# Token-major projections in chunks of 512 columns, in a transformer kernel of eleven stages on one core

## The reference

```
# first block, layer 0 (mix_0) and layer 1 (mix_1)
qa, ka, va, qb, kb, vb = jnp.split(xn @ w_in, splits, axis=-1)    # va: 256 columns, vb: 768
q, k, v = jnp.split(xn @ w_in, 3, axis=-1)                        # v: 1024 columns
# second block (mix_2)
hq, hf, hi, hgt, nq, kc, vc, ksl, vsl, kwn, vwn, ngate = jnp.split(h @ w_in[l], offsets, axis=-1)
                                                  # hi: 512, vsl and vwn: 128 each, ngate: 24 columns
```

## Time and profile before

| | |
|---|---|
| timed runs, median of 3 | 3481.54 us (3477.34 to 3484.66) |
| profiled execution, its span from first to last instruction | 3476.3 us |
| PE busy in it | 3343.7 us, 96% |
| DVE, ACT, POOL busy | 1999.1, 1753.2, 1211.2 us |
| mean granted clock of TensorE | 0.985 of full |
| `v_ab`, `v_c`, `tok_2` in the span | about 502 to 582, 1624 to 1671, 2341 to 2393 us |

### The profile page before, as it was taken

How to read it: one execution, slowest core, us unless ns; L and a number is a source line. 1 busy time by engine, 2 the same in 40 slices (tenths; PEclk the granted TensorE clock), 3 DMA queues, 4 the chain that set the end, 5 groups by cost and what they waited for, 6 DMA issues and landing times.

```text
span 3476.3 us, 49224 instructions
## 1 busy us (share of the span) xinstructions
PE 3343.7 (96%) x16800; PEld 2705.7 (78%) x16800; DVE 1999.1 (58%) x2493; ACT 1753.2 (50%) x2114; POOL 1211.2 (35%) x625
## 2 busy tenths in 40 slices
PE   8999999999999999999999999899889999999996
PEld 6888888678888788888678888688766788787774
DVE  4335672663354433541463333457776699888888
ACT  5552212645533555321545533423563688888883
POOL 3444441044444444444134444342203222222224
PEclk9999999999999999999999999999999999999998
DMA  3225321023244222443422233222002899999997
GB/s 125 96 95 171 112 100 37 2 85 97 97 150 141 85 97 97 151 132 110 128 72 95 96 94 103 76 95 82 31 1 77 333 402 414 408 410 401 393 397 307
DMA packets 128103, 555.40 MB, mean 160 GB/s; under 512 B 19344, under 2 KB 19600, under 8 KB 100112
## 3 DMA queue, kind: packets, MB, share of 16 engines
q1 hardware_dynamic: 112896, 520.59, 41.5%
q0 software_dynamic: 14976, 33.58, 2.6%
q10 hardware_dynamic: 144, 0.08, 0.0%
HBM read 531.62 MB, written 41.94 MB: 165 GB/s over the span
## 4 chain that ended last, share of the span: by engine, by line
PE 60%; issue 25%; POOL 7%; DVE 5%; ACT 2%; DMA 1%; POOLq 0%; DVEq 0%; SPq 0%; ACTq 0%
PE ps L731 17%; PE ps L733 16%; PE ps L732 16%; POOL w_lo L1762 7%; PE ps L1189 2%; PE ps L751 1%; PE ps L892 1%; PE ps L1268 1%; PE ps L917 1%; PE ps L902 1%; PE ps L1018 1%; PE ps L1000 1%; PE ps L979 0%; DMA big<-in_exp_gu 0%; PE ps L1208 0%
## 5 line engine op out<-in xcount | busy, mean ns | idle before, releaser
L1762 POOL TENSOR_TENSOR w_lo<-stage_buf,w_hi 128x1024 fp32r<-128x1024 f32 (+1 forms) x396 | 971.8, 2454 | 1554.9 <-ACT w_hi L1344 1554.9
L1344 ACT ACTIVATE w_hi<-stage_buf 128x1024 fp32r<-128x1024 f32 (+1 forms) x396 | 413.9, 1045 | 1254.9 <-PE ps L733 1204.8
L731 PE MATMUL ps<-x_hi,w_hi 128*128 128x512 f32 x1984 | 776.1, 391 | 8.7 <-POOL w_lo L1762 7.9
L732 PE MATMUL ps<-x_lo,w_hi 128*128 128x512 f32 x1984 | 774.9, 391 | 0.0
L733 PE MATMUL ps<-x_hi,w_lo 128*128 128x512 f32 x1984 | 774.5, 390 | 0.0
L731 PE MATMUL ps<-hid,w_hi 128*128 128x512 f32 x1312 | 519.0, 396 | 2.6 <-issue 1.7
L733 PE MATMUL ps<-hid,w_lo 128*128 128x512 f32 x1312 | 511.7, 390 | 0.0
L732 PE MATMUL ps<-hid,w_hi 128*128 128x512 f32 x1312 | 510.8, 389 | 0.0
L731 PEld LDWEIGHTS ps<-x_hi,w_hi 128*128 128x128 f32 x1984 | 374.2, 189 | 90.7 <-POOL w_lo L1762 9.6
L733 PEld LDWEIGHTS ps<-x_hi,w_lo 128*128 128x128 f32 x1984 | 374.3, 189 | 78.0
L732 PEld LDWEIGHTS ps<-x_lo,w_hi 128*128 128x128 f32 x1984 | 374.2, 189 | 77.5
(11 more groups left out here) (388 smaller groups left out, 5121.8 us busy)
## 6 DMA issues: line engine op xcount, KB each, us to landing
stage_buf<-in_gu SPq DMA_DIRECT2D x176, 512.0 KB, 3.3
big<-in_exp_gu SPq DMA_DIRECT2D x72, 1024.0 KB
h_buf<-in_exp_gu SPq DMA_DIRECT2D x72, 1024.0 KB
s_buf<-in_exp_dn SPq DMA_DIRECT2D x72, 1024.0 KB
slot_rows<-stage_buf SPq DMA_DIRECT2D x72, 512.0 KB
stage_buf<-in_down SPq DMA_DIRECT2D x64, 512.0 KB, 3.6
stage_buf<-in_down SPq DMA_DIRECT2D x32, 384.0 KB, 3.1
sil_buf<-in_ada SPq DMA_DIRECT2D x24, 512.0 KB, 4.1
```

The source lines that it names most:

```text
L731: nc.tensor.matmul(o, a_hi, b_hi, start=start, stop=False)
L732: nc.tensor.matmul(o, a_hi, b_lo, start=False, stop=False)
L1344: nc.scalar.activation(w_hi[s][:, 0:n], stage[s][:, 0:n], ACT.Copy).then_inc(upper_done, 1)
L1762: nc.gpsimd.tensor_tensor(w_lo[s][:, 0:n], stage[s][:, 0:n], w_hi[s][:, 0:n].bitcast(F32), ALU.subtract).then_inc(parted, 1)
```

## The change

The widths of the chunks come from a table: `v_ab` is cut in 256, 512 and 256 columns, `v_c` in 512 and 512, `tok_2` in 512 and 280 (the 256 value columns and the 24 gates, without the padding). A unit of a wide chunk holds two feature tiles and 512 (or 280) columns, so a wide chunk takes four units, and each unit feeds 24 matmuls. There are still eight units in each phase, of the same size. The `by_class` reading of the stationary operand stays as it is. PE's and DVE's waits count by the table. In mix_2 DVE has two evacuations instead of four, and the 24 gate columns are copied right behind the 256 value columns, ahead of `hgrn_keys`.

```diff
@@ -69,6 +69,18 @@
     PHASES += [(f"gu_{_l}_1", 2 * NF), (f"down_{_l}_1", KD * len(DOWN)), (f"pg_{_l}", 8), (f"pp_{_l}", 2)]
 PHASES += [("in_2", 20), ("tok_2", 8), ("cmp", 8), ("out_2", 8), ("shared", 6)]
 WHOLE = ("cmp", "shared")
+
+
+V_WIDTHS = {"v_ab": [256, 512, 256], "v_c": [512, 512], "tok_2": [512, 280]}
+CHUNKS = {}
+for _name, _widths in V_WIDTHS.items():
+    CHUNKS[_name], _at = [], 0
+    for _c, _w in enumerate(_widths):
+        _deep = 4 if _w == 256 else 2
+        CHUNKS[_name].append(dict(width=_w, deep=_deep, first=_at, units=KD // _deep, col=sum(_widths[:_c]),
+                                  by_class=_name == "v_ab" and _c > 0))
+        _at += KD // _deep
+    assert _at == 8
 BASE, CUT = {}, {}
 _at = _cut = 0
 for _name, _n in PHASES:
...
@@ -810,27 +822,25 @@
 
             def token_major(phase):
 
-                U, units = BASE[phase]
-
-                def some(x, k, t, c):
-                    if phase == "v_ab" and c > 0:
-                        return by_class(x[:, k, :])[:, t, :]
-                    return x[:, k, t * P:t * P + P]
-
-                for c in range(units // 2):
-
-                    pe.wait_ge(evac_done, U + 2 * c)
+                U = BASE[phase][0]
+                for c, ch in enumerate(CHUNKS[phase]):
+                    width, deep, first = ch["width"], ch["deep"], ch["first"]
+
+                    pe.wait_ge(evac_done, U if c == 0 else U + 2 + CHUNKS[phase][c - 1]["first"])
                     if c == 1 and phase == "tok_2":
                         pe.wait_ge(std_ready, NORM_N["first"] + 1)
                     if c == 1 and phase in ("v_ab", "v_c"):
                         pe.wait_ge(rcol_ready, 1 if phase == "v_ab" else 2)
-                    for s in range(2):
-                        pe.wait_ge(parted, CUT[phase] + 2 * c + s + 1)
-                        wh, wl = tiles(w_hi[s], 256), tiles(w_lo[s], 256)
+                    for n in range(ch["units"]):
+                        s = (first + n) % 2
+                        pe.wait_ge(parted, CUT[phase] + first + n + 1)
+                        wh, wl = (tiles(w[s][:, 0:deep * width], width) for w in (w_hi, w_lo))
                         for t in range(TT):
-                            for kk in range(KD // 2):
-                                k = 4 * s + kk
-                                last = three(ps[:, 4 * ((c + 1) % 2) + t, 0:256], some(x_hi, k, t, c), some(x_lo, k, t, c),
+                            for kk in range(deep):
+                                k = deep * n + kk
+                                hi, lo = (by_class(x[:, k, :])[:, t, :] if ch["by_class"] else x[:, k, t * P:t * P + P]
+                                          for x in (x_hi, x_lo))
+                                last = three(ps[:, 4 * ((c + 1) % 2) + t, 0:width], hi, lo,
                                              wh[:, kk, :], wl[:, kk, :], k == 0, k == KD - 1)
                         last.then_inc(units_done, 1)
 
...
@@ -2042,22 +2052,25 @@
                         ins = nc.vector.tensor_scalar(o, a, scale, None, ALU.mult)
                     ins.then_inc(evac_done, 1)
 
-            def token_units(phase, first, n, dst, pitch, width=256):
+            def token_units(phase, first, n, dst, pitch):
 
                 U = u(phase)
                 d = tiles(big[:, dst:dst + TT * pitch], pitch)
-                for m in range(n):
-                    c = first + m
-                    dve.wait_ge(units_done, U + 2 * c + 2)
+                for c in range(first, first + n):
+                    ch = CHUNKS[phase][c]
+                    width = ch["width"]
+                    dve.wait_ge(units_done, U + ch["first"] + ch["units"])
                     b = 4 * ((c + 1) % 2)
-                    o, a = d[:, :, m * 256:m * 256 + width], ps[:, b:b + 4, 0:width]
-                    if phase == "tok_2":
-                        ins = nc.vector.tensor_copy(o, a)
+                    if phase == "tok_2" and c == 1:
+                        nc.vector.tensor_copy(d, ps[:, b:b + 4, 0:pitch])
+                        ins = nc.vector.tensor_copy(gates, ps[:, b:b + 4, pitch:width])
+                    elif phase == "tok_2":
+                        ins = nc.vector.tensor_copy(d, ps[:, b:b + 4, 0:width])
                     else:
-                        r = rcol[:, 1 if phase == "v_ab" and c > 0 else 0, :, None].to_broadcast([P, TT, width])
-                        ins = nc.vector.tensor_tensor(o, a, r, ALU.mult)
+                        r = rcol[:, 1 if ch["by_class"] else 0, :, None].to_broadcast([P, TT, width])
+                        ins = nc.vector.tensor_tensor(d[:, :, ch["col"]:ch["col"] + width], ps[:, b:b + 4, 0:width], r, ALU.mult)
                     link(ins)
-                    dve.sem_inc(evac_done, 2)
+                    dve.sem_inc(evac_done, ch["units"])
 
             def folded(name):
 
...
@@ -2654,7 +2667,7 @@
                     rope_units("in_ab", 12, 2, 12 * T, 1.0)
                     rope_units("in_ab", 14, 6, 14 * T, 1.0, by_class)
                     columns(st)
-                    token_units("v_ab", 0, 4, 20 * T, D)
+                    token_units("v_ab", 0, 3, 20 * T, D)
                     dve.sem_inc(FOLDED["ab"]["qkv"], 1)
                     folded("ab")
                     operand("out_ab")
...
@@ -2665,7 +2678,7 @@
                     modulation(st)
                     copy_units("in_c", 8, 8, 8 * T)
                     columns(st)
-                    token_units("v_c", 0, 4, 16 * T, 2 * D)
+                    token_units("v_c", 0, 2, 16 * T, 2 * D)
                     dve.sem_inc(FOLDED["c"]["qkv"], 1)
                     folded("c")
                     operand("out_c")
...
@@ -2703,12 +2716,11 @@
                     dve.wait_ge(sum_ready, SUM_N["first"] + 1)
                     compress_blocks()
                     hgrn_gates()
-                    token_units("tok_2", 0, 2, R_VI, T)
+                    token_units("tok_2", 0, 1, R_VI, T)
                     first_norm()
-                    token_units("tok_2", 2, 1, R_VSW, 256)
+                    token_units("tok_2", 1, 1, R_VSW, 256)
                     hgrn_keys()
                     hgrn_first_levels()
-                    token_units("tok_2", 3, 1, R_GATE, 24, width=24)
                     hgrn()
                     gated()
                     operand("out_2")
...
@@ -2729,10 +2741,14 @@
         n // width, P, (k // P) * width)
 
 
-def _halves(w):
-
-    n, _, cols = (u := _units(w, 256)).shape
-    return np.ascontiguousarray(u.reshape(n, P, 2, cols // 2).transpose(0, 2, 1, 3)).reshape(2 * n, P, cols // 2)
+def _chunks(phase, w):
+
+    out = np.zeros((8, P, UNIT), np.float32)
+    for ch in CHUNKS[phase]:
+        n, deep, width = ch["units"], ch["deep"], ch["width"]
+        part = w[:, ch["col"]:ch["col"] + width].reshape(n, deep, P, width).transpose(0, 2, 1, 3)
+        out[ch["first"]:ch["first"] + n, :, 0:deep * width] = part.reshape(n, P, deep * width)
+    return out
 
 
 def _column(v):
```

More of the change, by code:

```diff
@@ L2810, in _lay_out @@
     a["in_ab"] = _units(np.concatenate([_heads(qa, order_a), qb, ka, kb], axis=1))
-    a["v_ab"] = _halves(np.concatenate([va, vb], axis=1))
+    a["v_ab"] = _chunks("v_ab", np.concatenate([va, vb], axis=1))
     w = f("w_out_ab")[0]
@@ L2814, in _lay_out @@
     w = f("w_in_c")[0]
-    a["in_c"], a["v_c"] = _units(w[:, :2048]), _halves(w[:, 2048:])
+    a["in_c"], a["v_c"] = _units(w[:, :2048]), _chunks("v_c", w[:, 2048:])
     a["out_c"] = _units(f("w_out_c")[0])
@@ L2829, in _lay_out @@
     a["in_2"] = _units(np.concatenate([hq, hf, hgt, _heads(nq, order_n), kc, vc, ks, kw], axis=1))
-    a["tok_2"] = _halves(np.concatenate([hi, vs, vw, np.pad(ng, ((0, 0), (0, 232)))], axis=1))
+    a["tok_2"] = _chunks("tok_2", np.concatenate([hi, vs, vw, ng], axis=1))
     a["cmp"] = np.stack([x for n in ("k", "v") for x in
```

## The result

The changed kernel takes **3455.7 us** (median of 4 runs, 3452.1 to 3458.7) where the kernel before took 3481.6 beside it (4 runs, 3477.3 to 3484.7). The ratio is 0.9929, with a 95% interval of 0.9915 to 0.9943: faster by 0.7%, 20 to 30 us. On another occasion it was 3454.0 against 3476.9, ratio 0.9928 (0.9914 to 0.9941). The forecast was 3453.4, or 28.1 us less; the medians say 25.9 and 22.9 less. The profiled execution has a span of 3454.5 us, 21.8 less than before's.

A forecast was written before the change was run, and what follows sets the result against it. It took TensorE, busy 96% of the span, as the main bound, with VectorE's list bounding the third mixer. Savings of 22.4 + 1.5 + 4.2 = 28.1 us gave 3453.4 us from 3481.5, range 3447 to 3463.

The forecast's parts named there:

- First mixer: By-class value chunks: strided load sets 0.233 us per matmul, so 96 matmuls instead of 192 save 22.4 us.
- Rival A: First mixer: load and product run in series at 512 columns, 0.446 us; 7.7 us saved in all, 3473.8 us; chance 0.10.
- Second mixer: Two chunks of 512: PE 2.56 us shorter, longer last evacuation costs 1.06, so 1.5 us less.
- side check: Second mixer: skill's lone-gap formula, 109 and 216 ns, would save 0.4 us before the evacuation; the stage would lose 0.6.
- Third mixer: Chunks of 512 and 280: DVE's waits shrink by 4.8 us, 0.6 charged for slow clock; 4.2 us less, bounds 2.5 and 5.0.
- Rival B: Third mixer follows PE in full: 11.8 us less instead of 4.2, 3445.8 us; chance 0.04.
- Rival C: Third mixer gives nothing, slow clock and preparation of weight units eating the gain: 3457.6 us; chance 0.03.
- The sum: Whole kernel: the three mixers' savings total 28.1 us, giving 3453.4 us, 0.8% faster; chance 0.80.
- Rival D: Recurrence: after 9 us idle PE's clock stays low through the stage, costing 54 us, 3507.4 us; chance 0.03.

The follow-up runs named there:

- e1_vab: Kernel before with only the first mixer's values in chunks of 256, 512, 256; second and third mixer keep four of 256: 3458.2 us, ratio 0.9937.
- e10_copy_old: Kernel before's 256-column chunks throughout, but the first mixer's by-class chunks read class-ordered copies written by ScalarE, without a stride: 3448.1 us, ratio 0.9905.
- e7_light: Changed kernel, but the third mixer's second chunk (280 columns) issues only the first of its three products per tile: 3455.6 us, one run.
- e3_tok: Kernel before with only the third mixer's phase in chunks of 512 and 280; the other two mixers keep four of 256: 3477.8 us, ratio 0.9999.
- e9_notok: Changed kernel with the third mixer back in its four chunks of 256 columns: 3459.2 us, ratio 0.9944 to the kernel before.
- e5_copy: Changed kernel, but ScalarE writes class-ordered copies of both operand halves, which the first mixer's by-class chunks read without a stride: 3437.9 us, ratio 0.9884.
- e6: Changed kernel plus 36 unused matmuls of 512 columns filling PE's idle time before the recurrence: 3456.5 us, ratio 0.9941 to the kernel before.
- after_again: The changed kernel unaltered, timed and profiled a second time beside the kernel before: 3454.0 us, ratio 0.9928.
- e11_stride2: Changed kernel, but the first mixer's by-class chunks read their stationary operand at stride 2 instead of 4, changing values: 3415.7 us, one run, total not compared.

## Why the prediction was right, step by step

**First mixer, 22.4 us expected.** Right: 67.20 - 44.96 = 22.24 us, shown by the evacuations of the changed kernel and again by e1_vab, timed at 18 to 26. The pitch of the wide by-class matmul is 22.68 / 96 = 0.236 us against the 0.233 taken. Rival A (load and product in series, 0.446) is out. That hardly anything is gained beyond the hidden load is confirmed by e10_copy_old. One reading was finer than its row: the starts of the one-column matmuls are given to 0.1 us, so their pitch is 0.23 to within 0.02, and "to the nanosecond" can't be said.

**Second mixer, 1.5 us expected.** Right in the trace: 2.5 from PE, 1.07 back for the longer evacuation. At L927, behind the DMA, 1.2 us is left (1680.82 - 1660.46 = 20.36, less the 19.15). The timed run of this part alone (0.9986 to 1.0003) can't show it. In the side check beside this term the two gaps differ by 2.5 ns and not 2.3, which makes 0.5 us and not 0.4; nothing hangs on it.

**Third mixer, 4.2 us expected (2.5 to 5.0).** The steps came as said: no wait of PE for DVE between chunks, the copies without a wait, the logarithm done early, the keys without a wait. Against the profiled execution of before it is 5.05, against the old chunks with the clock up 3.1. What I had not seen is that the rows of before I worked from, 0.99 us for PE and a clock of 0.52 in the earlier trace rows, hold a slow stretch that three other traces of the same chunks don't have. I charged half a slow stretch (0.6 us) to the new kernel, for an idle time of 2.1 us ahead of the third unit; that idle time was 1.58 us and the clock stayed at 1.00. The two errors pull opposite ways, so that 4.2 lies between 3.1 and 5.0 is in part luck. Rival B (PE in full, 11.8 us) is excluded by the 5.05 us itself, and by e7_light, where less work of PE moved nothing. Rival C (nothing) is what e3_tok's timed runs say and what e9_notok's don't; the rows exclude it as far as the end of this mixer's attention (4.7 us less on average there), but how much reaches the end of the kernel is not settled.

**The sum, 28.1 us expected, 22.9 and 25.9 in the medians.** Within the measurement (20 to 30), a little high. In the pair of profiled executions the lead was 23.3 us behind the first mixer (1.06 of it not the change's), 19.15 ahead of the second, 25.9 at 2405 us (of before) and 21.8 at the end. So 4 us went between the first two mixers, where nothing was changed. The loss that I followed to its place, 1.6 us between 680 and 694 us of before, is a stretch at 1.2 GHz in dense matmuls. Near 668 us, in the timeline of PE of the changed kernel:

```profile
667.64 0.63 PE L763 MATMUL ps<-x_hi,w_hi 128*128 128x512 f32 x1
668.07 0.63 PE L763 MATMUL ps<-x_hi,w_lo 128*128 128x512 f32 x1
...
671.04 0.39 PE L763 MATMUL ps<-x_lo,w_hi 128*128 128x512 f32 x1
671.26 0.39 PE L763 MATMUL ps<-x_hi,w_hi 128*128 128x512 f32 x1
```

The pitch there is 0.43 us instead of 0.227, for some eight matmuls. These windows show that one of the two executions can have such a stretch where the other has none. The first two are of the changed kernel, around the start of `v_ab` and at the matmuls just shown; the third is of before, around the start of `v_ab`:

```profile
499.00:502.40 3.40, 3.40 (x22) 3.32 (x21) 3.01 (x5) 1.06 (x1) 1.71 (x1) 1.00 0.37 142
...
668.00:671.50 3.50, 3.50 (x11) 2.69 (x10) 3.24 (x6) 1.06 (x3) 0.00 (x0) 0.57 0.00 0
```

```profile
501.00:504.40 3.40, 3.40 (x16) 3.40 (x17) 3.33 (x5) 0.00 (x0) 1.78 (x1) 0.55 0.10 25
```

Summed over windows of each trace, the time at the lower level was 104 us before and 118 and 126 in the two profiled executions of the changed kernel (112 to 125 in e1 to e3, e5, e6, e9). e1_vab and e9_notok have more of it than before too, with the old third mixer, so it is not that part's doing. A part of it costs nothing, like 3 us ahead of the recurrence without a matmul (2364 to 2367, clock 0.50). An estimate from the same windows, weighted with PE's busy share, is 66 us before and 74 and 78 after; with about half a microsecond lost for each, this could take up to 4 to 6 us. The timed executions point the same way: those of the changed kernel were granted a mean of 0.982, those of the kernel before in the first two groups 0.985, and before's own ran longer at a lower clock (3485.7 us for two at 0.982, 3472.3 for one at 0.987). Why the changed kernel's clock is lower is open, and that this is the missing 2 to 5 us is argued, not shown.

**Rival D, the clock in the recurrence.** In the windows from the start of the recurrence on, 189 us, of before and then of the changed kernel, the granted clock is 0.95 and 0.92:

```profile
2391.00:2580.00 189.00, 164.40 (x1311) 130.62 (x1311) 141.63 (x359) 108.24 (x244) 27.98 (x30) 0.95 0.09 29
```

```profile
2366.00:2555.00 189.00, 163.01 (x1276) 129.80 (x1276) 140.60 (x352) 107.31 (x241) 28.39 (x30) 0.92 0.09 29
```

It came back to the upper level after each slow stretch. Measured from the first row, the lead of 5.05 us at the first masked scores was 2.3 at the 32nd and 2.5 at the attention's last scores, so at most 2.7 us went, not the 54 of that rival; in after_again 4.8 of it was left at the 32nd.

## What to carry to other kernels

Before widening a matmul, ask what its pitch is made of. If a slow stationary load hides the product, as 0.233 us did at 1 column and at 256, then more columns are nearly free until the product is as long as the load. The better cure is to make the load fast: two copies of 1.1 us for each tile, in ScalarE's idle time, took 31.4 us off without any wide chunk, where the wide chunks alone took off 23 to 26, and with both the kernel takes 3437.9 us.

Read a stage's worth between two instructions on the engine that ends it, over several traces: timed totals of a 3.5 ms kernel can't tell 3 us from none, and a single profiled execution may hold a slow stretch that others lack. When an experiment changes values in a kernel that routes by them, count its blocks before believing its time.

## What the runs showed of the hardware

- With a stationary load of 4-byte values before each matmul of 256 columns, the pitch is the same at strides of 1 and 2 (0.120 us), and almost the same at 4 and 8 (0.232 and 0.241): a step, not a slope.
- The same idle time of PE (2.1 us for DVE before the third chunk) was followed by the lower clock in two traces and not in three others.
- ScalarE copied 128x512 values through a strided read in 1.11 us; an activation of the same size without a stride takes 0.69 in this trace (L1402 in e5_copy; it has another function and reads the matmul's results, so the stride is not the only difference).
- A by-class chunk of 512 columns took 22.4 us at a stride of 2 (e11_stride2) and 21.8 without (e5_copy), though at 256 columns the two are equal (11.51). Why is open.
